# Two HBM scratch buffers instead of one for the turned chunks of a two-layer encoder, and two landing semaphores in turn

## What is computed

```
layer 0: h = rms_norm(x);  proj = h @ w_in                      (2048 x 3584)
         mixer A: sliding-window attention, 16 heads of 64, 4 key/value heads, sinks, ALiBi
         mixer B: chunked gMLP gating, 8 groups of 128 channels
         x = x + [A, B] @ w_out
         x = x + (silu(h' @ w_gate) * (h' @ w_up)) @ w_down      (hidden 5632), h' = rms_norm(x)
layer 1: h = rms_norm(x);  q, k, v = h @ w_qkv                  (2048 x 6144)
         mixer C: stick-breaking attention, 16 heads of 128
         x = x + C @ w_out;  then the same feed-forward
```

## Time and profile before

| | |
|---|---|
| median of 3 runs | 2084.54 us (2084.04, 2084.54, 2084.89) |
| the profiled execution's own time | 2085.62 us |
| its span in the trace | 2083.8 us |
| granted TensorE clock | 1.0 throughout |
| busy: PE, PEld, DVE, ACT, POOL | 2076.4, 1720.9, 1217.7, 971.3, 149.8 us |
| moved by DMA | 447.37 MB, mean 215 GB/s |
| POOL's DMA queue | 51.08 MB, 9.3% of 16 engines |
| SP's DMA queue | 392.72 MB, 56.6% of 16 engines |

### The profile page before, as it was taken

One profiled execution on the slowest core, in us unless ns is written; L12 is line 12 of the kernel. 1 busy time (PEld: TensorE's weight loads), 2 busy tenths in 40 slices (PEclk: granted clock), 3 DMA queues, 4 the chain that ended last, 5 costly groups with the idle time before them and its releaser, 6 DMA issues.

```text
span 2083.8 us, 22669 instructions
## 1 busy us (share of the span) xinstructions
PE 2076.4 (100%) x9420; PEld 1720.9 (83%) x9420; DVE 1217.7 (58%) x1298; ACT 971.3 (47%) x1084; POOL 149.8 (7%) x251
## 2 busy tenths in 40 slices
PE   9999999999999999999999999999999999999999
PEld 8878888888888888888888888888888888888887
DVE  7776655555455554656666666655555455554654
ACT  6565554443444434445455455554443444434443
POOL 1010100000000000011110100100000000000010
PEclk9999999999999999999999999999999999999999
DMA  9666766765667656678766666776765667666673
GB/s 332 216 203 193 248 216 219 234 209 196 194 212 235 209 200 189 212 236 250 227 216 206 208 195 202 237 216 220 236 206 198 192 212 237 207 201 188 212 237 130
DMA packets 214567, 447.37 MB, mean 215 GB/s; under 512 B 10225, under 2 KB 10241, under 8 KB 214209
## 3 DMA queue, kind: packets, MB, share of 16 engines
q1 hardware_dynamic: 197600, 392.72, 56.6%
q0 software_dynamic: 16448, 51.08, 9.3%
q10 hardware_dynamic: 416, 2.13, 0.3%
HBM read 419.67 MB, written 26.21 MB: 214 GB/s over the span
## 4 chain that ended last, share of the span: by engine, by line
PE 97%; DMA 1%; DVE 1%; issue 0%; SPq 0%; ACT 0%; POOL 0%; DVEq 0%; POOLq 0%
PE acc L1101 32%; PE acc L1102 32%; PE acc L1107 32%; DMA raw<-in_w_in 1%; DMA spread<-blocks 0%; DMA blocks<-folded 0%; PE turn_zb L1220 0%; DVE w_lo L746 0%; PE turn_zb L1121 0%; PE turn_zb L1193 0%; PE turn_zb L1131 0%; PE turn_zb L1160 0%; PE turn_zb L1133 0%; PE turn_zb L1132 0%; PE turn_zb L1211 0%
## 5 line engine op out<-in xcount | busy, mean ns | idle before, releaser
L543 ACT ACTIVATE w_hi<-raw 128x1024 fp32r<-128x1024 f32 x744 | 786.9, 1059 | 982.7 <-PE acc L1107 977.7
L746 DVE TENSOR_TENSOR w_lo<-raw,w_hi 128x1024 fp32r<-128x1024 f32 x744 | 899.8, 1221 | 579.2 <-ACT w_hi L543 578.8
L1101 PE MATMUL acc<-w_hi,xT_hi 128*128 128x512 f32 x2016 | 786.4, 390 | 1.7 <-DVE xT_lo L806 1.1
L1102 PE MATMUL acc<-w_hi,xT_lo 128*128 128x512 f32 x2016 | 784.5, 389 | 0.0
L1107 PE MATMUL acc<-w_lo,xT_hi 128*128 128x512 f32 x2016 | 538.8, 389 | 0.0
L1101 PEld LDWEIGHTS acc<-w_hi,xT_hi 128*128 128x128 f32 x2016 | 378.4, 188 | 81.5 <-DVE xT_lo L806 1.6
L1107 PEld LDWEIGHTS acc<-w_lo,xT_hi 128*128 128x128 f32 x2016 | 378.4, 188 | 78.7
L1102 PEld LDWEIGHTS acc<-w_hi,xT_lo 128*128 128x128 f32 x2016 | 378.4, 188 | 77.9
L1101 PE MATMUL acc<-w_hi,m_hi 128*128 128x512 f32 x956 | 372.4, 390 | 0.0
L1102 PE MATMUL acc<-w_hi,m_lo 128*128 128x512 f32 x956 | 371.9, 389 | 0.0
L1107 PE MATMUL acc<-w_lo,m_hi 128*128 128x512 f32 x956 | 255.5, 389 | 0.0
(11 more groups left out here) (155 smaller groups left out, 531.6 us busy)
## 6 DMA issues: line engine op xcount, KB each, us to landing
raw<-in_w_gate SPq DMA_DIRECT2D x88, 1024.0 KB, 5.2
raw<-in_w_up SPq DMA_DIRECT2D x88, 1024.0 KB, 6.0
raw<-in_w_down SPq DMA_DIRECT2D x88, 1024.0 KB, 5.1
raw<-in_w_qkv SPq DMA_DIRECT2D x48, 1024.0 KB, 5.6
raw<-in_w_out SPq DMA_DIRECT2D x32, 1024.0 KB, 5.1
raw<-in_w_in SPq DMA_DIRECT2D x26, 1024.0 KB, 5.5
blocks<-folded POOLq DMA_DIRECT2D x42, 512.0 KB, 4.0
spread<-blocks POOLq DMA_DIRECT2D x168, 128.0 KB, 5.9
```

Source lines behind the costliest of these rows:

```text
L543: nc.scalar.activation(w_hi[:, h.slot, :, :], raw[:, h.raw_slot, 2 * h.part:2 * h.part + 2, :], ACTF.Copy).then_inc(hi_ready, 1)
L746: nc.vector.tensor_tensor(w_lo[:, h.slot, :, :], raw[:, h.raw_slot, 2 * h.part:2 * h.part + 2, :], f32(w_hi[:, h.slot, :, :]), ALU.subtrac ...
L1101: nc.tensor.matmul(dst, hi[:, h.k0 + k, at], wh, start=h.opens and k == 0, stop=False)
L1102: nc.tensor.matmul(dst, lo[:, h.k0 + k, at], wh, start=False, stop=False)
```

## The change

The HBM scratch `blocks` gets two halves used in turn. POOL no longer waits at the end of `bounce(F)` until its four spread DMAs have landed; before it writes chunk F it waits that chunk F - 2, whose half it overwrites, has come back. As two chunks' landings can now be in flight, they count on two semaphores in turn, and everybody who waits for a landing (ACT at two places, PE at one) waits on that of F's parity. The wait for `fold_out`, the wait for a free `spread` buffer, and the waits of DVE stay as they are.

```diff
-        fold_done, fold_out, fold_landed, fold_hi, fold_lo = (sem(n) for n in ("fold_done", "fold_out", "fold_landed", "fold_hi", "fold_lo"))
+        fold_done, fold_out, fold_hi, fold_lo = (sem(n) for n in ("fold_done", "fold_out", "fold_hi", "fold_lo"))
+
+        fold_landed = [sem(f"fold_landed{q}") for q in range(2)]
...
-        blocks = nc.dram_tensor("blocks", (TT, P, CH), F32, kind="Internal").ap()
+        blocks = nc.dram_tensor("blocks", (2, TT, P, CH), F32, kind="Internal").ap()
+
+        def landed(F):
+
+
+            return fold_landed[F % 2], 16 * QUARTERS * (F // 2 + 1)
...
                 pool.wait_ge(fold_done, F + 1)
-                pool.dma_start(blocks.rearrange("t p n -> p t n"), (p_folded if F < A_KV else folded)[:, :, :]).then_inc(fold_out, 16)
+                if F >= 2:
+                    pool.wait_ge(*landed(F - 2))
+                pool.dma_start(blocks[F % 2].rearrange("t p n -> p t n"), (p_folded if F < A_KV else folded)[:, :, :]).then_inc(fold_out, 16)
                 pool.wait_ge(fold_out, 16 * F + 16)
...
                 for b in range(QUARTERS):
                     pool.dma_start(back[b * BLK:(b + 1) * BLK].rearrange("j t a r -> j (t a) r"),
-                                   blocks[:, :, b * P:(b + 1) * P].rearrange("t (a j) r -> j (t a) r", a=QUARTERS)).then_inc(fold_landed, 16)
-                pool.wait_ge(fold_landed, 16 * QUARTERS * (F + 1))
+                                   blocks[F % 2, :, :, b * P:(b + 1) * P].rearrange("t (a j) r -> j (t a) r", a=QUARTERS)).then_inc(fold_landed[F % 2], 16)
...
-                act.wait_ge(fold_landed, 16 * QUARTERS * (F + 1))
+                act.wait_ge(*landed(F))
...
-                        act.wait_ge(fold_landed, 16 * QUARTERS * (F + 1))
+                        act.wait_ge(*landed(F))
...
-                        pe.wait_ge(fold_landed, 16 * QUARTERS * (g + 1))
+                        pe.wait_ge(*landed(g))
```

## The result

The changed kernel takes 2090.28 us (median of 10 runs, 2088.67 to 2092.88) where the kernel before, beside it on the same chip, takes 2084.94 (10 runs, 2084.04 to 2086.72). The ratio is 1.0027, 95% interval 1.0017 to 1.0036: slower, by some 5 us. The forecast was 2083.2 us with a range of 2082.3 to 2085.4, so time and sign are wrong.

A forecast was written before the change was run, and what follows sets the result against it. PE bounds the kernel, busy 2076.4 of 2083.8 us; only its 1.31 us wait for `xT_lo` at F = 21 would go, all else zero: 2084.54 - 1.31 = 2083.23 us, range 2082.3 to 2085.4.

The forecast's parts named there:

- The chain at F = 21: Out of F = 21 goes 1.64 us earlier, its spread lands earlier, and PE's 1.31 us wait for `xT_lo` goes whole.
- POOL's six waits for spreads: POOL's waits for a spread's landing, 39.6 us in all, forecast to fall to nearly nothing; five end before PE needs the chunk.
- The collision: Rival, chance 0.05: F = 22's earlier out delays F = 21's spread by 1.8 us, PE's stall grows to 3.2 us, time 2086.4.
- the prediction's bound: At F = 20, spread issue follows the out by 4.5 us, or 6.2 at the longest seen, so over by 968.9.
- The second semaphore and the second half of the scratch replace names and addresses: In each bounce on POOL: same five DMAs and as many waits, so neither gain nor loss.
- a new wait of PE behind a fold: Listed sign that the forecast is wrong: a new PE wait at any L1101 for a chunk turned by a fold.
- that very pattern at F = 21: Before the change, the out of F = 21 began 1.06 us behind a weight load and took 5.89 us.
- A loss would need a stall over three times the one there is: From the rival of something beyond 0.2%, chance 0.04: such a loss needs loads held up at several of six places.
- The old stall: PE's wait for DVE's `xT_lo` of F = 21, from 996.86 to 998.17, 1.31 us, forecast to go whole.
- the forecast's base: Median before of 2084.54 us, 1.08 us below the profiled execution, from which the 1.31 us were subtracted.
- the stall of 997: PE's 1.31 us wait for `xT_lo` near 997 us, the only listed PE wait hanging on a turned chunk.

The follow-up runs named there:

- experiment 8: Changed kernel plus five 512 KB HBM-to-HBM copies on POOL's queue between F = 3 and F = 4: 2084.45 us, ratio 0.9992.
- experiment 5: Kernel before with only the scratch of two halves used in turn, one landing semaphore, wait kept at bounce's end: 2085.87 us, ratio 1.0.
- experiment 7: Kernel before with POOL held up ahead of the out of F = 45 alone by 12 one-column memsets: 2085.26 us, ratio 0.9998.
- experiment 10: Kernel before with the out of F = 45 alone held back by four chained memsets of 256 columns: 2088.69 us, ratio 1.0015.
- experiment 12: Kernel before plus five 512 KB HBM-to-HBM copies on POOL's queue between F = 3 and F = 4: 2085.65 us, ratio 1.0002.
- experiment 6: Kernel before with only two landing semaphores in turn, one scratch, wait kept at bounce's end: 2093.33 us, ratio 1.0035.
- experiment 9: Kernel before with two halves, one landing semaphore, POOL waiting for F - 1's landings only ahead of F's spread: 2084.35 us, ratio 0.9996.
- experiment 11: Changed kernel with the landings on four semaphores in turn instead of two: 2092.57 us (one run).
- experiment 3: Changed kernel with one more POOL instruction, a one-column memset, at the end of each bounce: 2090.04 us (one run).
- experiment 2: Changed kernel with three more small DMAs of 8 KB at the start of POOL's queue: 2090.11 us, ratio 1.002.
- experiment 4: Changed kernel, two halves and two semaphores kept, with the wait for the landings back at each bounce's end: 2091.82 us, ratio 1.0035.

## Why the prediction was wrong

- **The chain at F = 21 was right, step by step.** Out at 974.88 (forecast 975.28; it stood 0.29 us behind its transpose, not 0.55), spread issued at 979.04 (979.52), landed at 988.31 (988.5), no wait at 997, 2.72 us from half to half. POOL's six waits for spreads, 39.6 us, are gone.
- **The collision didn't come.** The spread of F = 21 had landed 1.3 us before the out of F = 22 began (989.62). The out of F = 20, which now ran beside the spread of F = 19 and a weight load, took 7.42 us instead of 4.27 and delayed nobody. That is beyond the prediction's bound: 6.2 us from out to spread was called the longest seen, where the longest out of the trace, 6.4 us to its landing, gives 6.7. Experiment 8 has the overlap in full and is no slower.
- **The step that failed** is "The second semaphore and the second half of the scratch replace names and addresses ... this brings neither gain nor loss." For the half it holds (1.0, 0.9991 to 1.001). The second semaphore moves a pause of POOL on to F = 45, and alone it costs at least as much as the whole change (1.0035, 1.0023 to 1.0046). So a term put at nothing was some 5 us, and the sign that the prediction had named, a new wait of PE behind a fold, showed (2.3 us for `m_lo`).
- **What I passed over.** The waits of POOL held three rows beside the one that I read the earlier trace rows: issue twice at the out, once at the spread, once at a DMA of the result. I read the waits of the engine on the bound for what the change removes, and didn't ask what the idle times called issue on POOL were, nor where they fell. That would not have told that a semaphore moves them; it would have told that POOL has a stall of 1.4 us with a place of its own, and that an edit to its DMAs might move it on to a chunk without slack.
- **What it costs beyond its 1.4 us** was missing as a term. The out of F = 45, 0.55 us behind a 1 MB weight load instead of 0.59 us ahead of it, took 6.76 us, not 3.98. The prediction used that very pattern at F = 21 (out 1.06 us behind a load, 5.89 us) and didn't ask it of the other chunks that PE needs at once. The Trainium skill says of it that DMAs of all issuing engines run on the same 16 DMA engines and interleave (DMA: Bandwidth & Descriptors, Issuing engines are not separate DMA queues); the trace agrees in that the out beside the load took 2.8 us longer, and adds that a shift of 1.1 us in the order was enough for it.
- **"A loss would need a stall over three times the one there is"** ruled out what came, since it counted stalls alone. Behind a stall of 2.4 us PE also ran at half clock for 3.4 us, 1.7 us more. The old stall, 1.31 us, had no dip behind it. (Of that rival's neighbour, the collision, one sum is off too: 1.31 + 1.8 is a stall of 3.1 us, not 3.2.)
- **What stays open.** What in POOL's handling of DMAs makes the pause, and why its spacing goes with the number of landing semaphores (11.5, 11 and 9 bounces with 1, 2 and 4): no run opens POOL itself. Why the medians of after differ from before by 5.3 us in one comparison and 3.3 in the other: the profiled execution, at a mean granted clock of 0.999, is 1.3 us faster than its median, and the run at 0.998 was the slowest (2092.88), so more or longer dips are likely, but no profile of such a run of this kernel was taken. And part of the forecast's base was softer than it looked: the stall of 997 varies from execution to execution (none in the profiles of experiments 5, 7, 10 and 12 and 0.4 us in that of 6, though their out of F = 21 still waits for F = 20). The 1.31 us were read from one execution that was itself 1.08 us slower than the median from which they were subtracted, so less may have been there to win on average. Experiments 8 and 9, with the stall gone, lie 1.2 and 0.95 us below the medians beside them; neither interval tells that from nothing.

## What to carry to other kernels

An engine off the critical path may have rare pauses of its own, which cost nothing only as long as they fall on work with slack; look up each idle time called issue on the engine whose queue a change touches, with the chunk it falls on, and ask which chunk has no slack. To overlap a transfer with the one ahead, first ask whether moving the wait does it (experiment 9) before adding semaphores; it kept the pauses where they were. When a small change of order moves the time by more than its own size, compare the outs' places against the big loads and the granted clock behind each new stall.

## What the runs showed of the hardware

- **GpSimd pauses for up to 1.5 us before a DMA, rarely and at repeatable places.** From the semaphore to the out it takes 1.68 us instead of 0.29 (1.96 instead of 0.55 where POOL waits at the end of a bounce), and once 1.76 instead of 0.28 ahead of a spread. It can be shorter: 1.45 instead of 0.29 in experiment 11, and 0.98 instead of 0.29 at F = 11 in experiment 8. The places did not move with 46 more POOL instructions (experiment 3), with three small DMAs (2), with the addresses (5) or with overlap (4 beside after, 9 beside before); they did move with the number of landing semaphores (6, 11) and with 512 KB copies ahead (8, 12).
- **A second landing semaphore moved the pause, and the place decided the cost.** With it alone the kernel took 2093.33 us beside 2085.62 (experiment 6); with it and the copies, which kept the pause off F = 45, 2084.45 beside the same 2085.62 (8). The Trainium skill advises one semaphore per in-flight slot (DMA: Bandwidth & Descriptors, Why a DMA increments its semaphore by 16 and not by 1), because a count shared by two DMAs in flight can be reached by parts of both. That reason stands, and no run here tests it. Where the issuing engine asks for the landing ahead before it issues the next spread, no two spreads are in flight, and one semaphore was enough (2084.35 us, experiment 9).
- **Order against a load.** A 512 KB out takes 3.2 us at best and 4.0 in the median. Issued 0.59 us ahead of a 1 MB load it took 3.98 us (before, F = 45), 0.27 us ahead 5.97 (experiment 7), 0.55 us behind 6.76 (after), and 0.70 us behind 6.62 (experiment 10, where no pause of POOL's own is in play). Over all 14 profiles, the 66 outs issued between 0.35 us ahead of a load and 1.1 us behind one stood 6.0 us or more ahead of their spread, some 20 of them without a pause of POOL before them; of the 472 issued 0.5 to 0.9 us ahead, 441 stood less than 4.5 us ahead of theirs.
- **TensorE's clock around a stall.** In the profile of after the granted clock fell to 1.2 GHz 1.2 us behind the end of the 2.4 us stall and came back 3.4 us later, so that stall cost 4.1 us in all. The stalls of 1.9 and 3.0 us in experiment 6 and of 2.0 us in experiment 3 were followed by 3.4 us at the lower level too. In experiment 11 the clock fell inside the stall of 4.7 us, at 1270.6, and stayed low until 1277.4, 6.8 us; PE was back at work at 1273.43, so 4.0 of these cost matmul time. No dip came with the stall of 1.31 us before, nor with those of 1.3, 1.1 and 0.7 us in experiment 4.
